# Delta rule chunk stage on compact 64x64 blocks, one array quarter per product, four copies moved to ACT

## What is computed

```python
def wkv7_scan(r, w, k, v, kk, a):
    """state (B, H, N_v, N_k):  S_t = S_{t-1} (diag(w_t) - kk_t^T (a_t*kk_t)) + v_t k_t^T ;  y_t = S_t r_t"""
    def step(state, inp):
        r_t, w_t, k_t, v_t, kk_t, a_t = inp
        sk = jnp.einsum('bhvk,bhk->bhv', state, kk_t)
        state = (state * w_t[:, :, None, :]
                 - sk[..., None] * (a_t * kk_t)[:, :, None, :]
                 + v_t[..., None] * k_t[:, :, None, :])
        return state, jnp.einsum('bhvk,bhk->bhv', state, r_t)
```

## Time and profile before

| | us |
|---|---|
| median of 3 runs | 3296.72 |
| lowest, highest | 3277.16, 3298.33 |
| profiled execution: span | 3275.4 |
| PE busy | 3032.2 |
| DVE busy | 1772.5 |
| ACT busy | 1036.6 |
| POOL busy | 233.3 |

### The profile page before, as it was taken

How to read it: one execution, slowest core, us unless ns; L and a number is a source line. 1 busy time by engine, 2 the same in 40 slices (tenths; PEclk the granted TensorE clock), 3 DMA queues, 4 the chain that set the end, 5 groups by cost and what they waited for, 6 DMA issues and landing times.

```text
span 3275.4 us, 39457 instructions
## 1 busy us (share of the span) xinstructions
PE 3032.2 (93%) x15821; PEld 2493.1 (76%) x15821; DVE 1772.5 (54%) x2318; ACT 1036.6 (32%) x1399; POOL 233.3 (7%) x274
## 2 busy tenths in 40 slices
PE   7878999988989999979999989998979999989997
PEld 6767888766678887868877768887768868768886
DVE  6667666667566667483345443335573354443334
ACT  4533222233532223432223332223422123332222
POOL 3100000000000000020121000000020130000000
PEclk9989999887999999889999999999989999999999
DMA  4224555221035554120002323321210003322221
GB/s 151 73 65 136 174 165 175 88 74 43 1 116 170 167 172 139 55 72 1 1 8 88 108 77 99 100 92 60 90 47 1 1 7 97 103 77 97 95 97 57
DMA packets 239053, 281.63 MB, mean 86 GB/s; under 512 B 7492, under 2 KB 225928, under 8 KB 238920
## 3 DMA queue, kind: packets, MB, share of 16 engines
q1 hardware_dynamic: 225598, 227.48, 21.8%
q0 software_dynamic: 12960, 52.14, 5.4%
q10 hardware_dynamic: 362, 0.11, 0.0%
HBM read 277.58 MB, written 2.10 MB: 85 GB/s over the span
## 4 chain that ended last, share of the span: by engine, by line
PE 83%; DVE 11%; issue 3%; ACT 2%; POOL 1%; DVEq 0%; ACTq 0%; POOLq 0%
PE psum L1823 21%; PE psum L1824 21%; PE psum L1825 21%; PE psum L2106 5%; PE psum L2074 2%; DVE wlo L1188 2%; PE psum L2114 1%; PE psum L1885 1%; DVE mo L1565 1%; DVE rest L1202 1%; PE psum L2227 1%; DVE rest L1207 1%; PE psum L2223 1%; ACT whi L730 1%; PE psum L1972 1%
## 5 line engine op out<-in xcount | busy, mean ns | idle before, releaser
L1823 PE MATMUL psum<-hh,whi 128*128 128x512 f32 x2112 | 841.6, 398 | 87.8 <-DVE wlo L1188 49.7
L1824 PE MATMUL psum<-hl,whi 128*128 128x512 f32 x2112 | 834.5, 395 | 0.0
L1825 PE MATMUL psum<-hh,wlo 128*128 128x512 f32 x2112 | 832.8, 394 | 0.0
L1188 DVE TENSOR_TENSOR wlo<-raw,whi 128x2048 fp32r<-128x2048 f32 x224 | 525.6, 2346 | 509.7 <-ACT whi L730 509.2
L730 ACT ACTIVATE whi<-raw 128x2048 fp32r<-128x2048 f32 x224 | 427.7, 1909 | 600.4 <-PE psum L1825 575.1
L1823 PEld LDWEIGHTS psum<-hh,whi 128*128 128x128 f32 x2112 | 404.8, 192 | 190.4 <-DVE wlo L1188 55.1
L1823 PE MATMUL psum<-mh,whi 128*128 128x512 f32 (+1 forms) x1184 | 459.1, 388 | 20.2 <-DVE ml L1353 9.1
L1824 PEld LDWEIGHTS psum<-hl,whi 128*128 128x128 f32 x2112 | 404.8, 192 | 85.0 <-issue 1.2
L1825 PEld LDWEIGHTS psum<-hh,wlo 128*128 128x128 f32 x2112 | 404.0, 191 | 85.9
L1824 PE MATMUL psum<-ml,whi 128*128 128x512 f32 (+1 forms) x1184 | 457.1, 386 | 0.0
L1825 PE MATMUL psum<-mh,wlo 128*128 128x512 f32 (+1 forms) x1184 | 456.8, 386 | 0.0
(11 more groups left out here) (341 smaller groups left out, 3066.6 us busy)
## 6 DMA issues: line engine op xcount, KB each, us to landing
rest<-in_ada_w POOLq DMA_DIRECT2D x64, 768.0 KB, 5.3
raw<-in_w_gu SPq DMA_DIRECT2D x44, 1024.0 KB, 5.1
raw<-in_w_in SPq DMA_DIRECT2D x34, 1024.0 KB, 5.2
raw<-in_w_mlp_in SPq DMA_DIRECT2D x32, 1024.0 KB, 5.5
raw<-in_w_mlp_out SPq DMA_DIRECT2D x32, 1024.0 KB, 5.0
raw<-in_w_out SPq DMA_DIRECT2D x16, 1024.0 KB, 5.0
raw<-in_w_down SPq DMA_DIRECT2D x16, 1024.0 KB, 5.0
raw<-in_w_mem_kv SPq DMA_DIRECT2D x8, 1024.0 KB, 5.0
```

What stands on the lines that cost most here:

```text
L1188: dve.tensor_tensor(wlo[:, g % 2, :, :], raw[:, g % 2, :, :], f32(whi[:, g % 2, :, :]), ALU.subtract)\
L1823: pe.matmul(out, whi_, xhi, start=first, stop=False)
L1824: pe.matmul(out, whi_, xlo, start=False, stop=False)
L1825: return pe.matmul(out, wlo_, xhi, start=False, stop=last)
```

## The change

- LT, MT, MM, T1 and AK are kept as compact 64x64 blocks, [128 partitions, 2, 4, 64]. In MM, LT and AK the partitions carry the chunk c and the free index is (i, t); in MT and T1 the partitions carry the half i and the free index is (c, t).
- L and LT are both computed from the features (`squares_of`), 16 matmuls each of 64x64 by 64 columns in place of 8 products and 8 transposes. ACT copies LT (now unmasked); DVE masks L.
- LM, TR and MLM are 16 matmuls of 64x64 by 64 columns each, in place of 8. LM and TR keep the row half of c and alternate the column half of i; MLM keeps the row half of i and alternates the column half of c. TR is a matmul against the identity, of every level, the first among them; a last transposition TF of full width fills the diagonal blocks of a new 128x128 buffer MB, whose zeros POOL writes once per layer. WU and WT read MB.
- Akk and AkkV work on quarters too. Ark and Arb alternate i. The fillers stand behind MLM now; tok 2 stands behind TF, and the second Ark no longer stands behind z.
- NH goes over t outside, then i and c: it turns over the four quarters and writes two banks side by side. S alternates i, U alternates c. Y goes over t outside and alternates i. S waits for a new semaphore gs_made.
- ACT takes over four copies: KhT (tok 2), HS of both chunks, LT. In return DVE loses them. POOL's `pairup` loop is gone.

The core of the diff:

```diff
-FILL = [[("tok", 2)], [("Akk", 0)], [("tok", 3)], [("Akk", 1)], [], [("AkkV",)],
-        [], [("Ark", 0)], [], [("Arb", 0)], [("Arb", 1)]]
+FILL = [[], [("tok", 3)], [], [("Akk", 0), ("Akk", 1)], [], [("AkkV", 0), ("AkkV", 1)],
+        [], [("Ark", 0), ("Ark", 1)], [], [("Arb", 0), ("Arb", 1)], [("tok", 2)]]
...
+                pool.wait_ge(S("features"), 4 * l + 4)
+                pool.memset(MB, 0.0).then_inc(S("mb_zero"), 1)
...
-                for m in range(NT):
-                    if m:
-                        ready(pool, J["WT", l, m - 1])
-                    for i in range(2):
-                        hs = slice(4 * i, 4 * i + 4)
-                        evacuated(pool, J["LT", l, m, i])
-                        q.step(pool.tensor_tensor(MT[:, hs, :], LT[:, hs, :], bc(pairup[:, :]), ALU.mult))
-                        pool.tensor_tensor(MT[:, hs, :], bc(ident[:, :]), MT[:, hs, :], ALU.subtract).then_inc(S("mt_start"), 1)
...
+                    for i in range(2):
+                        j = J["LT", l, m, i]
+                        ready(act, j)
+                        if m:
+                            evacuated(act, J["U", l, m - 1, i])
+                            evacuated(act, J["U", l, m - 1, 1])
+                        free(act.activation(LT[:, i, :, :], four(j), ACT.Copy), j)
+                    token_major(0, KA[:, 0, :])
+                    token_major(1, BT)
+                    for n in range(len(LEVELS)):
+                        for c in range(2):
+                            j = J["TR", l, m, n, c]
+                            ready(act, j)
+                            free(act.activation(MT[:, c, :, :], four(j), ACT.Copy), j)
...
+                            token_major(3, VT)
...
+                    act.wait_ge(S("mb_zero"), l + 1)
...
+                    token_major(2, KhT)
...
+                    for c in range(2):
+                        j = J["NH", l, m, c]
+                        act.wait_ge(S("gs_made"), 2 * (NT * l + m) + c + 1)
+                        p = bank(j).rearrange("p (x j n) -> p x j n", x=2, j=4)
+                        free(act.activation(HS[:, c, :, :], p[:, 1, :, :], ACT.Copy), j)
...
+                            free(dve.tensor_tensor(AK[:, i, :, :], pc4(j), bc(strict2[:, :]), ALU.mult), j)
...
+                        free(dve.tensor_tensor(T1[:, i, :, :], pc4(j), bc(lvl[:, 0, :]), ALU.mult), j)
...
+                        dve.tensor_tensor(GS[:, c, :, :], bc(ident2[:, :]), p[:, 0, :, :], ALU.subtract)\
+                           .then_inc(S("gs_made"), 1)
...
+                def products(name, m, left, right):
+
+                    ms = slice(m * P, (m + 1) * P)
+                    p = [start(name, l, m, i) for i in range(2)]
                     for t in range(4):
-                        ins = pe.matmul(p[:, t * P:(t + 1) * P], left[a, t, ms], right[a, t, ms], start=True, stop=True)
-                    done(ins)
+                        for i in range(2):
+                            a = half[i]
+                            ins = pe.matmul(p[i][:, t * P:(t + 1) * P], left[a, t, ms], right[a, t, ms], start=True, stop=True)
+                            if t == 3:
+                                done(ins)
...
+                            p = [start("AkkV", l, m, c) for c in range(2)]
...
+                def squares_of(name, m, left, right):
...
                     for i in range(2):
-                        p = start(*key, i)
+                        a, p = half[i], start(name, l, m, i)
                         for t in range(4):
-                            ins = pe.transpose(p[0:rows, t * P:(t + 1) * P], src[:, 4 * i + t, :], ident[:, :])
+                            for c in range(2):
+                                s = slice(m * P + CH * c, m * P + CH * c + CH)
+                                ins = pe.matmul(p[chunk[c], t * CH:(t + 1) * CH], left[a, t, s], right[a, t, s],
+                                                start=True, stop=True)
                         done(ins)
...
+                def turned(m, n):
+
+                    for c in range(2):
+                        p = start("TR", l, m, n, c)
+                        for t in range(4):
+                            for i in range(2):
+                                ins = pe.matmul(p[half[i], t * CH:(t + 1) * CH], MM[chunk[c], i, t, :], ident2[chunk[c], :],
+                                                start=True, stop=True)
+                        done(ins)
...
+                    fill(m, [("tok", 0), ("tok", 1)])
+                    pe.wait_ge(S("inv_start"), 2 * (NT * l + m) + 2)
                     for i in range(2):
                         evacuated(pe, J["LT", l, m, i])
...
                     for n in range(len(LEVELS)):
+                        for i in range(2) if n else ():
+                            evacuated(pe, J["MLM", l, m, n - 1, i])
+                        for c in range(2):
+                            p = start("LM", l, m, n, c)
+                            for t in range(4):
+                                for i in range(2):
+                                    ins = pe.matmul(p[half[i], t * CH:(t + 1) * CH], LT[chunk[c], i, t, :], MM[chunk[c], i, t, :],
+                                                    start=True, stop=True)
+                            done(ins)
+                        turned(m, n)
+                        fill(m, FILL[2 * n])
+                        for c in range(2):
+                            evacuated(pe, J["LM", l, m, n, c])
+                            evacuated(pe, J["TR", l, m, n, c])
...
-                            blocks("LM", m, n, i, LT, MM)
...
-                            turned(MM, CH, "TR", l, m, n - 1)
...
-                            blocks("MLM", m, n, i, MT, T1)
+                            p = start("MLM", l, m, n, i)
+                            for t in range(4):
+                                for c in range(2):
+                                    ins = pe.matmul(p[chunk[c], t * CH:(t + 1) * CH], MT[half[i], c, t, :], T1[half[i], c, t, :],
+                                                    start=True, stop=True)
+                            done(ins)
                         fill(m, FILL[2 * n + 1])
...
-                    turned(MM, CH, "TR", l, m, len(LEVELS) - 1)
+                    for i in range(2):
+                        p = start("TF", l, m, i)
+                        for t in range(4):
+                            ins = pe.transpose(p[0:CH, t * P:(t + 1) * P], MM[:, i, t, :], ident[:, :])
+                        done(ins)
                     fill(m, FILL[-1])
...
+                    p = [start("NH", l, m, c) for c in range(2)]
...
+                        for i in range(2):
+                            for c in range(2):
+                                s = chunk[c]
+                                pe.matmul(p[c][half[i], g], WU[s, 4 * i + t, 0:HD], BT[s, head(i, t)], start=True, stop=True)
+                        for i in range(2):
...
+                                if (t, i) == (3, 1):
+                                    done(ins)
...
+                        pe.wait_ge(S("gs_made"), 2 * (NT * l + m) + c + 1)
+                        if cc:
+                            pe.wait_ge(S("state"), 16 * l + 2 * cc)
+                        p = [start("S", l, m, c, i) for i in range(2)]
...
-                                o = p[HD * i:HD * i + HD, :]
-                                pe.matmul(o[:, t * HD:(t + 1) * HD], WU[s, 4 * i + t, 0:HD], BT[s, head(i, t)],
-                                          start=True, stop=True)
-                                a = 4 * HD + t * HD
-                                pe.matmul(o[:, a:a + HD], KhT[s, head(i, t)], VT[s, head(i, t)], start=True, stop=False)
-                                ins = pe.matmul(o[:, a:a + HD], BT[s, head(i, t)], WU[s, 4 * i + t, HD:P],
-                                                start=False, stop=True)
-                        done(ins)
...
-                    fill(m, [("Ark", 1)])
...
-                            products("LT", m + 1, i, A2, KK)
+                        squares_of("L", m + 1, KK, A2)
+                        squares_of("LT", m + 1, A2, KK)
...
+                    p = [start("Y", l, m, i) for i in range(2)]
+                    for t in range(4):
+                        o = slice(t * P, (t + 1) * P)
+                        for i in range(2):
+                            pe.matmul(p[i][half[i], o], VT[:, head(i, t)], AR[:, 4 * i + t, :], start=True, stop=False)
+                        for i in range(2):
+                            pe.matmul(p[i][half[i], o], NU[:, 4 * i + t, :], AB[:, 4 * i + t, :], start=False, stop=False)
+                        for c in range(2):
+                            for i in range(2):
+                                a, x = half[i], t * P + CH * c
+                                ins = pe.matmul(p[i][a, x:x + CH], ST[a, (2 * m + c) % 3, t, :],
```

(3 more changed lines are left out.)

217 lines of the change are left out of this document (83 added, 134 removed).

## The result

The changed kernel takes 3122.18 us (median of four runs, 3120.49 to 3132.84), the kernel before 3295.31: ratio 0.9501, 95% interval 0.9458 to 0.9543. The forecast was 3170, range 3135 to 3258.

The account below looks back on a forecast made before the run. The prediction took PE, busy for 93% of the span, as the bound. Its terms summed to 117 us saved: 3160 from the profiled execution, 3180 from the median, so halfway, 3170 us, range 3135 to 3258.

Parts of the forecast that it names:

- Y: Output products: four pairs of heads take 3.87 us a block instead of 7.62, -30.0 us in all.
- The starts of the first blocks: Each layer's first block: the first level product starts 3.25 us earlier, twice, -6.5 us.
- Y to the levels: From output products to first level product: 2.3 us instead of 3.02, last waiting for ACT's copies, -4.3 us.
- the wait for GS: Before S in the tail: S must wait for GS, 0.77 us counted in full.
- Rival 3: Alternating column halves doesn't overlap: about +26 us a block, 3378 us; chance 0.03.
- rival 4: A wait taken as hidden adds 1 us or more per round or tail: 3225 us; chance 0.12.
- the levels: Five rounds of the inverse take 22.45 us a block instead of 31.09, at 29 ns a record: -69.1 us.
- The rounds with Akk: Level rounds whose filler is Akk or AkkV: 4.45 us each, against 4.25 for a plain round.
- NH: Tail, NH's start to U: 96 records at 29 ns take 2.78 us; 9.77 instead of 10.44, -5.3 us.
- U, S and the products before Y: End of the tail: 3.45 us a block instead of 3.69, -1.9 us.
- the base: Starting time for the saving: halfway between the profiled execution, 3277.16 us, and the median of three runs, 3296.72.
- rival 1: The clock falls to 1.2 GHz in some blocks, +25 us each: 3258 us taken; chance 0.18.

Follow-up runs that it names:

- same_rows: Kernel after, with LM and TR of chunk 0 issued first, then both of chunk 1: 3157.69 us, ratio 0.9614 to the kernel before.
- before_look2: The kernel before, unedited, run again with a profile: 3305.53 us.
- one_quarter: Kernel after, with the four heads of one array quarter in a row in the level products: 3200.94 us, ratio 0.9764 to the kernel before.
- four_all: Kernel after, with all 64x64 products turning over four quarters and both banks started together: 3115.2 us, ratio 0.9472 to the kernel before.
- crossed: Kernel after, with LM of one chunk issued beside TR of the other: 3117.52 us, ratio 0.9467 to the kernel before.
- warm: Kernel after, with unread transposes filling PE's waits before the first level in each layer's first block: 3120.66 us, ratio 0.9475 to before.

## Why the prediction was right or wrong

**Right.** The sign, the place (the stage, with alternating column halves), and Y: 3.87 forecast and 3.86 measured, with its -30.0. The starts of the first blocks, Y to the levels (2.3; 2.34), its releaser (ACT's copies), the wait for GS. Rival 3 fell where the rows said: alternating column halves overlap. So did rival 4.

**Wrong: the levels, "LM and TR issue for 1.86".** This is the step that failed. The term took 29 ns a record throughout, as if only two column halves could run beside each other. The 64 records take 1.35 us, since PE takes tiles of the other row half early at each of the three changes; same_rows takes two of the three away and gives 1.69 and a round of 4.17. That is 0.51 less, but MLM starts only 0.30 earlier (2.25 behind LM0 instead of 2.55): from the end of ACT's second copy to MLM it takes 0.26 us where the forecast had 0.08. MLM's own records (0.76 us from first to last start, not 0.93) and DVE's two operations, which follow at 0.34 us and not at 0.42, give the other 0.13, and the round is 3.82 and not 4.25. The rounds with Akk are 3.82 too and not 4.45: PE had room for it. Together -2.14 a block, 17 us, of which 11 were given back by the clock in the first blocks. The table's -78.2 holds 2.5 more that are losses of the kernel before in three of its blocks (33.9 twice and 34.94 instead of 33.41).

**Wrong: NH, "29 taken, the nearest row; the other end gives 11 us more".** The other end was right, 14.8 ns, and the term is -16.1 instead of -5.3. The bound had it; the choice of the nearest row, made with two halves only, was the error. The Trainium skill ("TensorE: Matmul & The Clock Gate", Part 1) says that two matmul starts never come closer than about 25 ns; by this NH would have taken 2.4 us, an estimate from that figure. The trace disagrees: 1.41.

**Wrong: "U, S and the products before Y: 3.45".** 2.55; U's 32 records take 0.76 us and the 64 of L and LT 1.34, as MLM and as LM with TR do, and the first records of L start among the last of S: the same look-ahead. That four quarters were allowed for NH alone, as a bound, and for no other group, is one reason why the range's low end (3160 - 25) was too high: those groups carried 5 more in U to Y and up to 17 in the levels. The 25 is not the sum of its terms either: the good ends given a size there are 11 (NH) and 6 (changes of shape).

**Wrong: the base.** "I can't tell which of the two levels the next kernel falls on." The traces show two places where the time of a run differs. One lies ahead of the stage and in both kernels: near 780 us the clock is low for 44 us in eight of the nineteen profiles and for 20 to 31 in the others, and the stage's first product starts at 1445 or at 1433 to 1436 us. The profiled executions of before and of after both have the long stretch, so their difference is free of it; but that of after was the slowest of its four runs, and the median is 10.7 us lower. The other place is inside the stage that was to be replaced: before_look2 lost 31 us more there than the first profile, which had lost 3 in one block. The median of before lies 18 us above its profiled run, and the forecast added half of that. That these 18 us were lost inside the stage, and taken away by the change, is an inference from before_look2: no run of before between 3278 and 3305 us was profiled. The row that hinted at it stood in the prediction (0.55 at full business), used only against the change.

**Missed the other way:** the first blocks. The forecast had rival 1 at 0.18; it happened in small: the low clock cost 4.5 and 6.0 us there.

In sum: 117 forecast; +9 net in the levels, +11 NH, +5 U to Y, +2 elsewhere make 144 for the profiled pair. The medians differ by 173: 18 more because the median of before lies above its profiled run (half of it was in the forecast), and 11 because the median of after lies below its own. So the result is 48 us under the forecast: 27 for the terms, 10 for the other half of the base, 11 for the runs of after. The last is chance, the profiled execution being the slowest of its four, and no term of the prediction.

## What to carry to other kernels

Small tiles in different quarters of TensorE's array run beside each other, and the order in the program sets the pace: 58 ns a record in one quarter, 29 in two column halves, 15 in four quarters, with some four tiles of look-ahead blurring the edges; so write the loops with the quarters innermost before anything is reshaped (Y's order alone gave 34 us, 26 of them in the stage). Once PE is fast, a round is a chain of hand-overs: feeding two engines alternately (0.4 us a round), or one wait less in front of a matmul (0.11), gave more here than faster issue (0.04). When runs of the kernel before spread, look in which stretch, before choosing the base of a forecast, and do so for the changed kernel's profiled execution too.

## What the runs showed of the hardware that was not expected

- 64x64 products start every 14.8 ns over four quarters (96 in 1.41 us).
- PE starts tiles ahead of their written order when these lie in another quarter: 5 to 6 ns behind a predecessor, three or four places early; a change of row half in mid-stream saves 0.17 us. The Trainium skill ("TensorE: Matmul & The Clock Gate", Part 3) has matmuls start strictly in order; the rows of one_quarter and of the round above disagree.
- The granted clock falls to 0.5 at a busy PE: 58 us of 82 at 81.52 busy. How long it stays low differed with the order of the same 64x64 tiles: in the first blocks 26 to 28 us in one_quarter, 21 and 37 in same_rows, 13 to 18 in the kernel after, 6 to 7 in four_all and crossed. The order is not all of it: warm, with the order of the kernel after, had 27 us once. The cause was not settled.
- Faster rounds showed idle times of PE of about 1 us that nothing in the profile releases; open as well.
